# Two hybrid layers and a recurrent block: branch products taken out of the accumulators ahead of a modulation row, and the first two output products interleaved

## The reference, cut to what matters

```python
mod = silu(c) @ ada_w + ada_b                       # 6 x 1024 values of a layer
sh_m, sc_m, g_m, sh_f, sc_f, g_f = split(mod, 6)
h = rms_norm(x, norm_mix_g) * (1 + sc_m) + sh_m
proj = h @ w_in                                     # q, k, v of three attentions, three gates ga, gb, gc
...
merged = (sigmoid(ga) * (o_na @ w_br_na)
          + sigmoid(gb) * (o_mla @ w_br_mla)
          + sigmoid(gc) * (o_gqa @ w_br_gqa))
x = x + g_m * (merged @ w_out)
h = rms_norm(x, norm_ffn_g) * (1 + sc_f) + sh_f
x = x + g_f * ((silu(gate) * up) @ ffn_w_down)      # gate, up = h @ ffn_w_gate_up
```

## Time and profile before

| | |
|---|---|
| median of 3 runs | 2891.52 us (2891.1 to 2896.4) |
| the profiled execution's own time | 2892.69 us |
| its span in the profile | 2890.9 us |
| mean granted TensorE clock | 0.996 of full |
| PE busy | 2839.6 us, 98% of the span |
| PE weight loads busy | 2247.1 us, 78% |
| DVE busy | 1564.2 us, 54% |
| POOL busy | 1669.2 us, 58% |
| ACT busy | 681.5 us, 24% |

### The profile page before, as it was taken

How to read it: one execution, slowest core, us unless ns; L and a number is a source line. 1 busy time by engine, 2 the same in 40 slices (tenths; PEclk the granted TensorE clock), 3 DMA queues, 4 the chain that set the end, 5 groups by cost and what they waited for, 6 DMA issues and landing times.

```text
span 2890.9 us, 44712 instructions
## 1 busy us (share of the span) xinstructions
PE 2839.6 (98%) x18182; PEld 2247.1 (78%) x18182; DVE 1564.2 (54%) x2327; ACT 681.5 (24%) x1162; POOL 1669.2 (58%) x1340
## 2 busy tenths in 40 slices
PE   7999999999999999999999999999999999999998
PEld 5766787888877767778888877877877787788886
DVE  7788876554225675444332375655565456562342
ACT  2444212000013443111000033333333423310000
POOL 6434577887765234586777754444344534676674
PEclk9999999999999999999999999999999999999999
DMA  9423543444324112132223321122112112222221
GB/s 305 134 93 125 196 164 121 145 146 152 131 95 94 35 61 66 64 119 88 94 94 102 103 77 49 62 69 70 54 64 68 63 54 69 81 95 95 97 100 59
DMA packets 102372, 285.50 MB, mean 99 GB/s; under 512 B 26030, under 2 KB 37038, under 8 KB 101934
## 3 DMA queue, kind: packets, MB, share of 16 engines
q1 hardware_dynamic: 85280, 274.68, 28.1%
q10 hardware_dynamic: 16910, 8.28, 1.4%
HBM read 280.76 MB, written 6.06 MB: 99 GB/s over the span
## 4 chain that ended last, share of the span: by engine, by line
PE 90%; DVE 7%; issue 1%; ACT 1%; DMA 0%; SPq 0%; DVEq 0%; POOL 0%; ACTq 0%; POOLq 0%
PE ps L338 25%; PE ps L339 24%; PE ps L340 24%; PE ps L1328 3%; PE ps L1148 3%; PE ps L1158 2%; PE ps L1168 2%; PE ps L1373 1%; DVE first_mod L1642 1%; DVE work L1607 1%; PE ps L982 1%; DVE hR L1614 1%; PE ps L1450 0%; DVE mg L1731 0%; PE ps L1292 0%
## 5 line engine op out<-in xcount | busy, mean ns | idle before, releaser
L563 POOL TENSOR_TENSOR wR<-raw,wR 128x512 fp32r<-128x512 f32 (+1 forms) x866 | 1199.0, 1404 | 37.6
L559 POOL CAST wR<-raw 128x1024 fp32r<-128x1024 f32 (+4 forms) x470 | 476.3, 1013 | 1152.5 <-PE ps L340 1024.7
L338 PE MATMUL ps<-hR,wR 128*128 128x512 f32 x2224 | 902.9, 406 | 11.9 <-DVE hR L1663 11.9
L339 PE MATMUL ps<-hR,wR 128*128 128x512 f32 x2224 | 869.2, 391 | 0.0
L340 PE MATMUL ps<-hR,wR 128*128 128x512 f32 x2224 | 868.9, 391 | 0.0
L338 PEld LDWEIGHTS ps<-hR,wR 128*128 128x128 f32 x2224 | 418.8, 188 | 116.6 <-issue 19.6
L340 PEld LDWEIGHTS ps<-hR,wR 128*128 128x128 f32 x2224 | 418.5, 188 | 89.5
L339 PEld LDWEIGHTS ps<-hR,wR 128*128 128x128 f32 x2224 | 419.2, 189 | 82.4 <-issue 4.8
L1621 DVE SCALAR_TENSOR_TENSOR xT<-ps,lm,xT 128x512 f32<-128x512 f32 x32 | 24.0, 751 | 215.3 <-PE ps L340 215.2
L338 PE MATMUL ps<-act_f,wR 128*128 128x512 f32 x352 | 137.7, 391 | 0.0
L340 PE MATMUL ps<-act_f,wR 128*128 128x512 f32 x352 | 136.9, 389 | 0.0
(11 more groups left out here) (383 smaller groups left out, 4112.4 us busy)
## 6 DMA issues: line engine op xcount, KB each, us to landing
raw<-in_weights_dram SPq DMA_DIRECT2D x468, 512.0 KB, 3.3
first_mod<-in_weights_dram SPq DMA_DIRECT2D x16, 512.0 KB, 10.4
raw<-in_weights_dram SPq DMA_DIRECT2D x50, 128.0 KB, 2.4
raw<-in_weights_dram SPq DMA_DIRECT2D x16, 256.0 KB, 3.0
bias_copies<-bias_rows ACTq DMA_DIRECT2D x2, 1905.0 KB, 10.3
bias<-bias_copies ACTq DMA_DIRECT2D x16, 224.0 KB, 7.3
raw<-in_weights_dram SPq DMA_DIRECT2D x8, 384.0 KB, 10.6
xT<-in_x_dram SPq DMA_DIRECT2D x1, 2048.0 KB, 9.4
```

The costliest lines, as they stand in the source:

```text
L338: mm(out, w_hi, r_hi, start=first, stop=False)
L339: mm(out, w_hi, r_lo, start=False, stop=False)
L559: nc.gpsimd.tensor_copy(wR[:, u, 0, 0:cols], raw[:, r % RING, 0:cols]).then_inc(hi_done, 1)
L563: ins = nc.gpsimd.tensor_tensor(wR[:, u, 1, part], raw[:, r % RING, part], wR[:, u, 0, part], ALU.subtract)
```

## The change

It has two parts. In `vector`, for the first layer, `post` of those late `na` products that are followed by a product of fewer than 8 steps now stands ahead of the step's modulation row. In the tensor program, in both layers, out0 and out1 are both claimed first (tile and bank of each), then run six steps each, then two more each; out2 to out7 run as before.

```diff
@@ tensor program, after the attention of each layer
-                for u in range(KD):
-                    slot, bank = need_tile(Count(TI + G_OUT + u)), claim(Count(PR + P_OUT + u))
-                    for k in range(KD):
+                def out_steps(u, slot, bank, ks):
+
+                    for k in ks:
                         if u == KD - 1 and k == KD - 1:
                             first_sums(R + 5, 2 * l + 1)
                         if u == 0:
                             pe.wait_ge(mg_ready, KD * l + k + 2)
                         mm = three_passes(MM, ps[:, bank, :], weight(slot, 0, k * P), weight(slot, 1, k * P),
                                           mg[:, 0, k, :], mg[:, 1, k, :], k == 0, k == KD - 1)
-                    mm.then_inc(tile_used, 1)
+                    return mm
+
+                outs = [(need_tile(Count(TI + G_OUT + u)), claim(Count(PR + P_OUT + u))) for u in range(2)]
+                for u in range(2):
+                    out_steps(u, *outs[u], range(KD - 2))
+                for u in range(2):
+                    out_steps(u, *outs[u], range(KD - 2, KD)).then_inc(tile_used, 1)
+                for u in range(2, KD):
+                    out_steps(u, need_tile(Count(TI + G_OUT + u)), claim(Count(PR + P_OUT + u)), range(KD)).then_inc(tile_used, 1)
@@ vector program, attention steps
                     behind(s)
+                    late = [p for p, early in ENDS[s] if not early and PRODS[p][0] in GATE_OF]
+                    first = [p for p in late if PRODS[p][0] == "na" and PRODS[p + 1][2] < KD]
+                    for p in first:
+                        post(p)
                     if l == 0:
                         rows_done = modulate(rows_done, DUE["step", s])
-                    for p, early in ENDS[s]:
-                        if not early and PRODS[p][0] in GATE_OF:
+                    for p in late:
+                        if p not in first:
                             post(p)
```

## The result

The changed kernel takes 2897.22 us in the median of 11 runs (2896.29 to 2899.91), the kernel before 2891.52 us (11 runs, 2891.06 to 2896.4). The ratio is 1.0017, with a 95% interval of 1.0009 to 1.0025. So it is slower, by less than the 0.2% that I had set as the bound, and the interval excludes no change at all. Its profiled execution took 2896.53 us, with a span of 2894.7; before, 2892.69 and 2890.9.

What follows compares the result with a forecast made beforehand. It took PE, busy 2839.6 of 2890.9 us, to bound the kernel. Attention gaps -2.2, first-layer output products +3.1, second-layer +0.8 and clock +1.6 summed to +3.3 us, 2894.8 us, range 2890.5 to 2898.0.

Steps and rivals of the forecast that it cites:

- What bounds the kernel: Whole kernel: PE, busy 2839.6 of 2890.9 us, so the change can win or lose almost only PE's standing time.
- Part one, -2.2 us: First-layer attention: PE's gaps before three small products fall from 0.99 to 0.26 us, 0.73 us gained each, -2.2 us.
- a row of 1.14 us fits in with 1 us to spare: DVE in attention: the modulation row behind post stays hidden in DVE's 2.11 us wait for the next scores.
- The gain lasts to the output products: Attention to output products: DVE's and POOL's work hangs on PE, so it moves along by 2.2 us.
- rivals 4 and 5: Attention to output products: POOL's tiles paced by transfers, +6.9 us, chance 0.06; moved post's gain lost again, +5.5 us, chance 0.08.
- Output products of the first layer, +3.1 us: Start of out0: 1.11 us lateness from `mg[7]` goes, 4.25 us from waiting for out1's tile comes, net +3.1 us.
- Rival 2: First-layer output products: only out1's bank holds out0, not its tile; net +0.9 us there, sum -0.5 us; chance 0.08.
- Second layer, +0.8 us: Second-layer output products: 0.44 us from `mg[7]` goes, 1.25 us from waiting for DVE's bank comes, net +0.8 us.
- The clock, +1.6 us, bounds 0 and 3: Behind the first-layer stall: TensorE's clock falls from 2.4 to 1.2 GHz, +1.6 us, bounds 0 and 3 us.
- rival 1: Behind the first-layer stall the clock stays up, everything else as forecast: +1.7 us, 2893.2 us; chance 0.24.
- Out2's bank: First-layer output products: out2's bank is freed 0.2 us before PE needs it; if not, it costs a tenth.
- The sum: Whole kernel: all terms together +3.3 us, 2894.8 us applied to the median; chance 0.52.

Runs made afterwards that it cites:

- part one alone: Kernel before, with only post of the three na products moved ahead of the modulation row, output products as before; 2891.02 us, ratio 0.9992.
- part two alone: Changed kernel with post put back behind the modulation rows, both claims still ahead of out0; 2899.78 us, ratio 1.0025 against the kernel before.
- only the bank first: Changed kernel, but out1's tile is waited for only after out0's six steps, its bank still ahead; 2893.28 us, ratio 1.0005 against the kernel before.
- only the tile first: Changed kernel, but out1's bank is claimed only after out0's six steps, its tile still ahead; 2896.94 us, ratio 1.0016 against the kernel before.
- PE kept at work: Changed kernel with 16 unread matmuls on ones put ahead of out0 in the first layer; 2895.02 us, ratio 1.0010 against the kernel before.
- late claim: Changed kernel, but out1's tile and bank are claimed only after out0's six steps; 2889.65 and 2889.69 us, ratios 0.9990 and 0.9989 against the kernel before.
- late claim without part one: Changed kernel with out1 claimed after out0's six steps and post put back behind the modulation rows; 2891.48 us, ratio 0.9991 against the kernel before.

## Why the prediction was right, point by point

- **What bounds the kernel.** Right: all that was found lies in gaps of PE at the places of the diff and in the clock behind one of them, but for 0.4 us lost in the attention behind the moved instructions.
- **Part one, -2.2 us.** Right in mechanism, each gap to 0.26 us as forecast; the sum was mis-sized at -1.8. What failed is the step "a row of 1.14 us fits in with 1 us to spare", which took all durations over unchanged from their old places. The row grew to 1.71 us and left 0.47; it stayed hidden even so. What reached PE is 0.31 us at a neighbour, an instruction that grew from 0.68 to 0.99 us, and 0.11 us that was not traced.
- **The gain lasts to the output products.** Right, shown by part one alone and part two alone. With that rivals 4 and 5 fall: POOL's gap is 4.2 us whether PE comes 1.9 us earlier or not, and output 1 is 82.69 us behind part one.
- **Output products of the first layer, +3.1 us.** Right to a tenth: with the clock held up it is 85.83 - 82.70 = +3.1. In the first profile of the changed kernel it is 0.2 more, since POOL's tile came that much later. Rival 2 (the bank alone) is what the kernel with only the bank first would have been, +0.99 against my +0.9; in the changed kernel the tile ended last.
- **Second layer, +0.8 us.** Measured +0.9, DVE's bank ending last, as stated.
- **The clock, +1.6 us, bounds 0 and 3.** It fell in all four profiles in which PE stood still for about 4 us (changed twice, part two alone, only the tile first), so rival 1 falls. Against PE kept at work it cost 1.45, 2.6 and 2.4 us. The bounds held, and 1.6 is right for the short form and 0.8 to 1 us too little for the long one. Nothing here says which form an execution takes, so it is luck that the profile of the first result shows the short one. The Trainium skill ("TensorE: Matmul & The Clock Gate", section "HAM oscillation — how this bites in real kernels") says that an engine which waits between tiles starts the next one throttled. The four stalls of about 4 us agree with it; behind the 1.85 us stall of the kernel with only the bank first the clock stayed up.
- **Out2's bank.** Right: its first matmuls show no gap in the changed kernel.
- **The sum.** +3.3 us against +3.85 and +4.8 by stretches and +5.7 and +4.6 by medians; 2894.8 us against 2897.22, inside 2890.5 to 2898.0. Part one brought 0.4 less, the stall cost up to 0.2 more, the clock from 0.15 less to 1 more. The rest of the first median, 0.9 us at the least, was not traced.

## What to carry to other kernels

Interleaving two accumulations hides a wait for an operand only if the second one's own claims come where it starts, not ahead of the first: read for each resource when it was ready before, and compare that with the new place of its wait. An operation that frees a buffer belongs ahead of bulk work on its engine where a short product follows; elsewhere in this kernel the same move was worth nothing. A stall of PE is to be priced with the slow matmuls behind it, which here added 1.45 to 2.6 us to a stall that cost 3.1, and an instruction moved beside another engine's is not as long as it was in its old place.

## What the runs showed that I had not expected

The clock fell in the middle of steady work too. In the profile of part one alone, PE was busy without a break, with many 128x1 sums of squares just before (line 1121 and 1122), and then ran at half the clock for 3.4 us, which cost 8 matmuls 0.2 us each. Stretches of PE in that profile, before and after the fall:

```profile
943.00:950.00 7.00, 7.00 (x51) 1.00 0.08 29
...
951.30:954.70 3.40, 3.40 (x9) 0.51 0.00 0
```

The starts of the kernel scatter in the same way: the wait for scores that stands at 183.9 to 184.1 us in ten of the twelve profiles comes at 186.9 and 186.8 us in the other two (late claim, and late claim without part one). In these two the granted clock was 0.72 from 64 to 70 us, where the second profile of the late claim shows 1.00. Its one profile would have made the late claim look no better than the kernel before (spans 2890.7 and 2890.9 us), while stretches and medians have it 3 us ahead.
